# A triangular inverse packed to 64 columns a chunk, on quarters of the matrix engine

## What is computed

```
a_mat = jnp.where(strict, jnp.einsum("bnhid,bnhjd->bnhij", kb, kc) * gamma, 0.0)
lhs = a_mat + jnp.eye(c, dtype=a_mat.dtype)
rhs = jnp.concatenate([vc * bc[..., None], kb * jnp.exp(decay)[..., None]], axis=-1)
sol = lax.linalg.triangular_solve(lhs, rhs, left_side=True, lower=True, unit_diagonal=True)
```

## Time and profile before

| | us |
|---|---|
| median of 3 runs (1599.14 to 1600.18) | 1600.07 |
| the profiled execution | 1601.17 |
| its span on the core | 1599.4 |
| PE busy, share of the span | 1569.8 (98%) |
| DVE, ACT, POOL busy | 912.6, 687.6, 160.7 |
| granted clock, mean | 0.997 |
| the loop over units, first to last record on PE | 195.9 to 268.0 |

### The profile page before, as it was taken

How to read it: one execution, slowest core, us unless ns; L and a number is a source line. 1 busy time by engine, 2 the same in 40 slices (tenths; PEclk the granted TensorE clock), 3 DMA queues, 4 the chain that set the end, 5 groups by cost and what they waited for, 6 DMA issues and landing times.

```text
span 1599.4 us, 21522 instructions
## 1 busy us (share of the span) xinstructions
PE 1569.8 (98%) x7488; PEld 1303.5 (82%) x7488; DVE 912.6 (57%) x1318; ACT 687.6 (43%) x1001; POOL 160.7 (10%) x101
## 2 busy tenths in 40 slices
PE   6999999999999999999999999999999999999997
PEld 5888798888788888888788888888888888888886
DVE  5569887865754234443477666666456544444332
ACT  6735656554644223333255554444224434443221
POOL 3444585300000000000000000000000000000000
PEclk9999999999999999999999999999999999999998
DMA  7522100132132332322233333333232332232332
GB/s 271 187 80 67 54 1 28 40 106 79 45 114 92 105 99 85 103 98 88 82 96 95 96 97 98 99 99 106 93 104 79 106 103 93 92 105 78 101 97 79
DMA packets 45665, 149.50 MB, mean 93 GB/s; under 512 B 4784, under 2 KB 5936, under 8 KB 45616
## 3 DMA queue, kind: packets, MB, share of 16 engines
q1 hardware_dynamic: 42240, 139.90, 27.2%
q10 hardware_dynamic: 3376, 8.95, 1.6%
HBM read 146.47 MB, written 2.10 MB: 93 GB/s over the span
## 4 chain that ended last, share of the span: by engine, by line
PE 94%; DVE 3%; DMA 1%; ACT 1%; issue 0%; SPq 0%; DVEq 0%; ACTq 0%
PE acc L633 85%; DMA raw<-panels_a 1%; PE acc L878 1%; PE acc L918 1%; DVE c_acc L2127 1%; PE acc L890 1%; DVE w_lo L1995 1%; PE acc L1126 0%; PE acc L1147 0%; PE acc L807 0%; PE acc L949 0%; PE acc L708 0%; PE acc L974 0%; DVE x L2702 0%; DVE d_score_a L2219 0%
## 5 line engine op out<-in xcount | busy, mean ns | idle before, releaser
L633 PE MATMUL acc<-h_hi,w_hi 128*128 128x512 f32 x1248 | 491.3, 394 | 1.2 <-DVE w_lo L2003 0.7
L633 PE MATMUL acc<-h_hi,w_lo 128*128 128x512 f32 x1248 | 485.9, 389 | 0.0
L633 PE MATMUL acc<-h_lo,w_hi 128*128 128x512 f32 x1248 | 485.8, 389 | 0.0
L2003 DVE TENSOR_TENSOR w_lo<-raw,w_hi 128x1024 fp32r<-128x1024 f32 (+2 forms) x241 | 281.6, 1171 | 81.8 <-ACT w_hi L1397 57.7
L1397 ACT ACTIVATE w_hi<-raw 128x1024 fp32r<-128x1024 f32 (+2 forms) x241 | 242.0, 1008 | 177.2 <-PE acc L633 86.1
L633 PEld LDWEIGHTS acc<-h_hi,w_hi 128*128 128x128 f32 x1248 | 234.4, 188 | 51.6 <-issue 3.5
L633 PEld LDWEIGHTS acc<-h_hi,w_lo 128*128 128x128 f32 x1248 | 234.3, 188 | 49.1
L633 PEld LDWEIGHTS acc<-h_lo,w_hi 128*128 128x128 f32 x1248 | 234.5, 188 | 48.1 <-issue 1.0
L2405 DVE TENSOR_TENSOR x<-x,acc 128x512 f32 x32 | 22.0, 688 | 136.0 <-PE acc L633 135.5
L633 PE MATMUL acc<-u_hi,w_hi 128*128 128x512 f32 x256 | 99.6, 389 | 0.0
L633 PE MATMUL acc<-u_lo,w_hi 128*128 128x512 f32 x256 | 99.6, 389 | 0.0
(11 more groups left out here) (400 smaller groups left out, 2317.2 us busy)
## 6 DMA issues: line engine op xcount, KB each, us to landing
raw<-panels_a SPq DMA_DIRECT2D x112, 512.0 KB, 3.2
raw<-panels_b SPq DMA_DIRECT2D x68, 512.0 KB, 3.2
raw<-mix SPq DMA_DIRECT2D x48, 448.0 KB, 3.4
raw<-mix SPq DMA_DIRECT2D x16, 512.0 KB, 3.6
raw<-down SPq DMA_DIRECT2D x16, 384.0 KB, 3.1
raw<-down SPq DMA_DIRECT2D x16, 320.0 KB, 2.8
x<-xT ACTq DMA_DIRECT2D x4, 1024.0 KB, 9.5
x_rows<-xN ACTq DMA_DIRECT2D x2, 1024.0 KB, 9.3
```

The costliest lines, as they stand in the source:

```text
L633: mm = e.matmul(out, w[:, w_at:w_at + wn], a, start=first and n == 0, stop=last and n == 2)
L2003: TTn(lo, raw, k.w_hi[:, ahead.slot(w)].bitcast(F32), ALU.subtract).then_inc(k.s_split_done, 1)
```

## The change

The inverse is kept for its two diagonal blocks of 64 only, as long as the level is under 6: the block of rows 0 to 63 and the block of rows 64 to 127 lie in the same 64 columns, on their own partitions. So a head's X has 256 columns (g_xp), its transpose too (g_xtp), and so have A (g_ap) and the masked A (g_b).

- Products and updates for u < 20 are eight fp32 matmuls instead of four. Each has 64 rows and 64 weight columns and moves 32 columns; the two blocks of a chunk come one behind the other, on rows and output partitions 0 to 63 and then 64 to 127, into the same PSUM bank.
- The turn is eight ordinary fp32 matmuls with 64x64 of the identity instead of four transposes.
- The last level (u >= 20) takes A's corner block directly: its mask step on POOL goes away, its product is four 64x64 matmuls moving 64 columns, and so is its update.
- Elementwise work halves: the mask 128x256, the copy of P 128x128 (64x256 at the last level), the subtraction 128x128, the copy of the turned inverse 128x128 (128x256 at level 1, two of 64x256 at level 5).
- Added on ACT: eight 64x256 copies that pack A, ahead of L1586; the first X is taken out of PSUM in eight copies of 64x256 instead of four of 128x512.
- PE's order in iteration u becomes: `power_product(u+1)`, update(u), `turn_inverse(u-1)`, front(u), turned(u). ACT's order stays.

```diff
...
 
 REST, CKV, CQ, UG, Z = 0, 1, 2, 4, 8
 UNITS = (LEVELS - 1) * HEADS
+W64, LAST = TT * 64, (LEVELS - 2) * HEADS
 WT_BANKS, GO_BANKS = (6, 7, 1, 2), (2, 0, 2, 0)
 PAIRS, BEAT = TT * HEADS, 3
 
...
     "out_row ").split())}
 
 ACT_ONCE = {n: i + 1 for i, n in enumerate((
-    "xk_sq d_gates_tok beta_done sp_exp xk_std dec_exp k_root dk_raw d_std go_std aq_std ").split())}
+    "xk_sq d_gates_tok beta_done sp_exp xk_std dec_exp k_root at_packed dk_raw d_std go_std aq_std ").split())}
 
 DVE_ONCE = {n: i + 1 for i, n in enumerate((
     "sp_in xk_inv g_ready dec_copied br qe dv_done d_inv dk_done c_bias go_bias go_inv "
...
     k.w_hi, _ = sb("w_hi", SPLIT * PANEL, F32R)
     k.x, a = sb("x", KT * T)
     k.g_at, b = sb("g_at", HEADS * T, at=a - KT * T * 4)
-    k.g_b, _ = sb("g_b", 4 * T, at=b)
     k.g_o, _ = sb("g_o", HEADS * T, at=b)
+    k.g_b, _ = sb("g_b", 4 * W64, at=b)
     k.d_qi, b = sb("d_qi", 2 * T, at=b)
+    k.g_ap, b = sb("g_ap", HEADS * W64, at=b)
     k.const, _ = sb("const", NCONST)
     k.vec, _ = sb("vec", NVEC)
     k.eps, _ = sb("eps", 4)
...
     k.qkv, a = sb("qkv", 12 * T, at=r0)
     k.g_qk, a = sb("g_qk", HEADS * T, at=a)
     k.d_relu, _ = sb("d_relu", HEADS * T, at=a)
+    k.g_xp, b = sb("g_xp", HEADS * W64, at=a)
+    k.g_xtp, _ = sb("g_xtp", HEADS * W64, at=b)
     k.g_x, a = sb("g_x", HEADS * T, at=a)
     k.g_xt, a = sb("g_xt", HEADS * T, at=a)
     k.g_kdec, a = sb("g_kdec", HEADS * T, at=a)
...
     return ap.rearrange("p (b s) -> p b s", s=1 << lev)
 
 
+def rows64(b):
+
+    return slice(64 * b, 64 * b + 64)
+
+
+def diag(buf, h, b):
+
+    return til(buf, h)[rows64(b), :].rearrange("p (c t) -> p c t", c=TT)[:, :, rows64(b)]
+
+
 def til(buf, j, n=1, w=T):
 
     return buf[:, j * w:(j + n) * w]
...
     def masked(u):
 
         h, lev = u % HEADS, 1 + u // HEADS
-        mask = k.const[:, C_LEV + lev * P:C_LEV + (lev + 1) * P].unsqueeze(1).broadcast_to([P, TT, P])
+        mask = k.const[:, C_LEV + lev * P:C_LEV + lev * P + 64].unsqueeze(1).broadcast_to([P, TT, 64])
         if u >= 4:
             e.wait_ge(k.s_p_mm, u - 3)
         else:
-            e.wait_ge(k.s_at_done, h + 1)
+            e.wait_ge(k.s_act_once, ACT_ONCE["at_packed"])
             e.wait_ge(k.s_idx_mm, 3 * HEADS)
             e.wait_ge(k.s_ld_masks, 16)
-        TTn(til(k.g_b, u % 4).rearrange("p (c i) -> p c i", c=TT), til(k.g_at, h).rearrange("p (c i) -> p c i", c=TT),
-            mask, ALU.mult).then_inc(k.s_bt_done, 1)
+        TTn(til(k.g_b, u % 4, w=W64).rearrange("p (c i) -> p c i", c=TT),
+            til(k.g_ap, h, w=W64).rearrange("p (c i) -> p c i", c=TT), mask, ALU.mult).then_inc(k.s_bt_done, 1)
 
     def conv_add(n):
 
...
         if p >= first:
             conv_add(p - first)
     for u in range(UNITS):
-        masked(u)
+        if u < LAST:
+            masked(u)
         conv_add(early - first + u)
     for n in range(early - first + UNITS, CONV_PARTS):
         conv_add(n)
...
     e.wait_ge(k.s_dve_once, DVE_ONCE["dk_done"])
     def power_product(u):
 
-        h, b = u % HEADS, (u % 4) * T
-        e.wait_ge(k.s_bt_done, u + 1)
+        h, lev = u % HEADS, 1 + u // HEADS
+        if u < LAST:
+            e.wait_ge(k.s_bt_done, u + 1)
         if u < HEADS:
             e.wait_ge(k.s_x_first, u + 1)
         else:
             e.wait_ge(k.s_x_done, u - 3)
         if u >= 2:
             e.wait_ge(k.s_p_copied, u - 1)
-        lev = 1 + u // HEADS
         for c in range(TT):
-            at = c * P
-            mm = e.matmul(packed(k.ps[u % 2][:, c * 64:(c + 1) * 64], lev), k.g_b[:, b + at:b + at + P],
-                          halves(til(k.g_x, h)[:, at:at + P], lev)[:, 0], start=True, stop=True)
+            x = k.g_xp[:, h * W64 + c * 64:h * W64 + (c + 1) * 64]
+            if u >= LAST:
+                mm = e.matmul(k.ps[u % 2][rows64(1), c * 64:(c + 1) * 64],
+                              k.g_at[rows64(0), h * T + c * P + 64:h * T + (c + 1) * P], x[rows64(0), :], start=True, stop=True)
+                continue
+            for b in range(2):
+                mm = e.matmul(packed(k.ps[u % 2][rows64(b), c * 32:(c + 1) * 32], lev),
+                              k.g_b[rows64(b), (u % 4) * W64 + c * 64:(u % 4) * W64 + (c + 1) * 64],
+                              halves(x[rows64(b), :], lev)[:, 0], start=True, stop=True)
         mm.then_inc(k.s_p_mm, 1)
+
+    def update(u):
+
+        h, lev, at = u % HEADS, 1 + u // HEADS, (u % 2) * T
+        e.wait_ge(k.s_p_copied, u + 1)
+        if u >= 2:
+            e.wait_ge(k.s_x_done, u - 1)
+        if u >= HEADS:
+            e.wait_ge(k.s_xt_done, u - HEADS + 1)
+        if LAST <= u < UNITS - 2:
+            e.wait_ge(k.s_xt_done, u - 1)
+        for c in range(TT):
+            if u >= LAST:
+                mm = e.matmul(k.ps[4 + u % 2][rows64(0), c * 64:(c + 1) * 64], k.g_p[rows64(1), at + c * 64:at + (c + 1) * 64],
+                              k.g_xt[rows64(1), h * T + c * P + 64:h * T + (c + 1) * P], start=True, stop=True)
+                continue
+            for b in range(2):
+                if lev == 1:
+                    xt = k.g_xt[rows64(b), h * T + c * P + 64 * b:h * T + c * P + 64 * b + 64]
+                else:
+                    xt = k.g_xtp[rows64(b), h * W64 + c * 64:h * W64 + (c + 1) * 64]
+                mm = e.matmul(k.ps[2 + u % 2][rows64(b), c * 32:(c + 1) * 32], xt, k.g_p[rows64(b), at + c * 32:at + (c + 1) * 32],
+                              start=True, stop=True)
+        mm.then_inc(k.s_xp_mm, 1)
 
     def turn_inverse(u):
 
...
         if u >= 2:
             e.wait_ge(k.s_xt_done, u - 1)
         for c in range(TT):
-            at = c * P
-            mm = e.transpose(k.ps[4 + u % 2][:, at:at + P], til(k.g_x, h)[:, at:at + P], ident)
+            for b in range(2):
+                mm = e.matmul(k.ps[4 + u % 2][rows64(b), c * 64:(c + 1) * 64],
+                              k.g_xp[rows64(b), h * W64 + c * 64:h * W64 + (c + 1) * 64], ident[rows64(b), rows64(b)],
+                              start=True, stop=True)
         mm.then_inc(k.s_xt_mm, 1)
 
     power_product(0)
     for u in range(UNITS):
-        h, last, b = u % HEADS, u >= UNITS - HEADS, (u % 2) * T
         if u + 1 < UNITS:
             power_product(u + 1)
+        update(u)
+        if 1 <= u <= LAST:
+            turn_inverse(u - 1)
         front(*FILL[u])
         if u in TURNS:
             name, th, src = TURNS[u]
             turned(name, th, src, src + th + 1 if src == 8 else 1)
-        e.wait_ge(k.s_p_copied, u + 1)
-        if u >= 2:
-            e.wait_ge(k.s_x_done, u - 1)
-        if u >= HEADS:
-            e.wait_ge(k.s_xt_done, u - HEADS + 1)
-        if last:
-
-            if u < UNITS - 2:
-                e.wait_ge(k.s_xt_done, u - 1)
-            for c in range(TT):
-                at = c * P
-                mm = e.matmul(k.ps[4 + u % 2][0:64, c * 64:(c + 1) * 64], k.g_p[:, b + c * 64:b + (c + 1) * 64],
-                              til(k.g_xt, h)[:, at + 64:at + P], start=True, stop=True)
-        else:
-            for c in range(TT):
-                at = c * P
-                mm = e.matmul(k.ps[2 + u % 2][:, c * 64:(c + 1) * 64], til(k.g_xt, h)[:, at:at + P],
-                              k.g_p[:, b + c * 64:b + (c + 1) * 64], start=True, stop=True)
-        mm.then_inc(k.s_xp_mm, 1)
-        if 1 <= u <= UNITS - HEADS:
-            turn_inverse(u - 1)
     left("z3")
     left("kt3")
 
...
     leave("ckv", til(k.proj, CKV))
     round_lead()
     conv_part()
+    for h in range(HEADS):
+        e.wait_ge(k.s_at_done, h + 1)
+        for b in range(2):
+            ins = A(til(k.g_ap, h, w=W64)[rows64(b), :].rearrange("p (c t) -> p c t", c=TT), diag(k.g_at, h, b), ACT.Copy)
+    ins.then_inc(k.s_act_once, 1)
     e.wait_ge(k.s_pe_once, PE_ONCE["dk_mm"])
     A(k.d_rk[:], k.ps[4][:], ACT.Square).then_inc(k.s_d_sq, 1)
     A(k.d_k[0:64, :], k.ps[4][0:64, :], ACT.Copy)
...
     turned_value(0)
     for h in range(HEADS):
         e.wait_ge(k.s_x_turned, h + 1)
-        A(til(k.g_x, h), k.ps[h][:], ACT.Copy).then_inc(k.s_x_first, 1)
+        for b in range(2):
+            ins = A(til(k.g_xp, h, w=W64)[rows64(b), :].rearrange("p (c t) -> p c t", c=TT), diag(k.ps[h], 0, b), ACT.Copy)
+        ins.then_inc(k.s_x_first, 1)
     for u in range(UNITS):
 
         e.wait_ge(k.s_p_mm, u + 1)
         if u >= 2:
             e.wait_ge(k.s_xp_mm, u - 1)
-        A(k.g_p[:, (u % 2) * T:(u % 2) * T + T // 2], k.ps[u % 2][:, 0:T // 2], ACT.Copy).then_inc(k.s_p_copied, 1)
+        rows, n = (slice(0, P), P) if u < LAST else (rows64(1), W64)
+        A(k.g_p[rows, (u % 2) * T:(u % 2) * T + n], k.ps[u % 2][rows, 0:n], ACT.Copy).then_inc(k.s_p_copied, 1)
         if parts.at() < CONV_PARTS:
             conv_part()
         if FILL[u][2] == KT:
...
                 turned_value(h)
             else:
                 turned_key(h)
-        if 0 <= u - 2 < UNITS - HEADS:
-
```

(21 more changed lines are left out.)

## The result

| | before | changed |
|---|---|---|
| median of 6 runs | 1600.12 us | 1628.78 us |
| lowest to highest | 1599.14 to 1601.49 | 1609.49 to 1636.95 |
| ratio, 95% interval | | 1.0155 [1.0128, 1.0183] |
| the profiled execution | 1601.17 | 1631.03 |
| its span, granted clock | 1599.4, 0.997 | 1629.2, 0.978 |

The ratios and intervals, here and among the experiments, leave out runs over 1.5% above the fastest of the same kernel (here 1636.95); the medians keep them.

What follows compares the result with a forecast made beforehand. PE was taken to bound the kernel, carrying 94% of the chain. Start -0.5 and loop +5.0 made +4.5 on the profiled 1601.17, so 1605.7, or 1604.6 us for the median; range for 8 in 10: 1595.5 to 1616.

Steps and rivals of the forecast that it cites:

- What bounds the kernel, and the price of quarter work: Loop: PE carries 94% of the chain; product, update and turn 0.46 us each, plain unit 2.46 against 2.87.
- The switches: PE going from whole to part array and back in each unit: 0.30 us, bounds 0.1 and 0.5.
- the rivals in which the halves take turns: PE's quarter pairs: streams take turns, +7.4, 1612 us (15%); or no overlap at all, +22, 1627 us (8%).
- What the new order uncovers: Loop: PE waits behind ACT's bursts for P's copy; intervals 5.20 us at keys, 4.20 at values.
- the wait for z3's copy: Loop's end, after update(23) and front(23): PE waits for ACT's copy of z3, 0.16 + 0.69 us more.
- The sum at full clock: update(2) to L1044: 68.39 us against 63.39, 5.0 more.
- the wait for a turn copy in the last level: Placed at update(21), behind ACT's burst of u = 19, making u = 20 take 2.60 us.
- The start: Ahead of the loop: DVE saves 2.0 us, x(0) at 200.1, update(2) at 204.15, 0.5 earlier.
- What costs nothing: Eight packing copies on ACT, 2.4 to 3.4 us, hidden in its 7.47 us wait before L1586; shorter POOL and DVE work.
- the rival in which it falls: Loop: new waits drop PE to 1.2 GHz in the 11 plain units, +27, 1632 us; chance 3%.
- the prediction's own sign of being wrong: In the trace: the counted waits missing, a product's rows at 1.1 or more, or granted clock below 1.00 in the loop.
- Slower: Whole kernel: slower by over 3.2 us, 68%; within 21%, faster 11%.

Runs made afterwards that it cites:

- e4: Changed kernel plus useless whole-array fp32 matmuls on PE where it waits behind ACT's bursts of scaled copies; 1614.42 us, 1.0100 of before.
- e9: e8 plus e4's filler matmuls in PE's waits behind ACT's bursts; 1601.73 us, 1.0010 of before.
- e8: Changed kernel with front(0) ahead of the first product, front(1) ahead of update(0), last updates in banks 2 and 3; 1609.22 us, 1.0037 of before.
- e3: Changed kernel with ACT's scaled copies of a turned unit one iteration later, behind the copy of P; 1602.11 us, 1.0024 of before.
- e1: Changed kernel with PE's old order restored, packing and halved elementwise work kept; 1599.42 us, 0.9992 of before.
- e5: e1 with the last level's updates written to banks 2 and 3, not those of the turned inverse; 1591.14 us, 0.9939 of before.
- e6: e5 with front(0) ahead of the first product and front(1) ahead of update(0), where PE waited at the start; 1589.06 us, 0.9927 of before.
- e2: Kernel before with only the new PE order, matmuls still whole-array; 1621.73 us, 1.0132 of before.

## Why the prediction was wrong, point by point

- *What bounds the kernel, and the price of quarter work*: right. 0.46 to 0.48 for each product and update, 2.44 for a plain unit against 2.46. The switches cost less than taken: turn and front together took 1.49 where 1.54 was counted. The pairs overlapped although they write to one PSUM bank. That settles the rivals in which the halves take turns: with streams in turn a turn would have cost 0.39 on top of the 0.46 and its switch, and it took 0.59 with the switch. The rule of TensorEngine Tiling (Array Packing), section Gotcha 1: PSUM Pressure, of the Trainium skill, didn't bind for two row halves that write to different partitions of a bank.
- *What the new order uncovers*: right, with 2.01 us of wait at the key bursts of u = 10, 13 and 16 where 2.1 was counted, and 5.05 for 5.20; values 4.12 or 4.13 (e4, e9) for 4.20; the wait for z3's copy 0.69, as given.
- *The sum at full clock*: right, in part because misses cancel. e4 has the changed kernel's path with its clock at 1.00 from 205 on. In it update(2) begins at 206.51 and the old L1044 (its L1076) at 274.57: 68.06 us, where the sum has 68.39. One term was misplaced: the wait for a turn copy in the last level stands at update(20), not update(21). So u = 19 took 7.26 in e4 where 5.45 stood, and the other terms together 2.1 less than they were given. e8 and e9 at 0.997 or more took 1600.5 to 1604.6, where 1602 to 1604 was expected of e8.
- *The start*: DVE's six taps fell from 8.97 to 5.92, 3.05 saved where 2.0 was taken and 2.6 was the bound; the masks take 0.735 and not 0.64 (rows below). 0.81 of that went unused, because x(0) waited so long for update(0); it began at 199.86, where 200.1 was forecast. But update(2) began at 207.90 and not at 204.15, with the clock down from 198 on. What I left out is that product(0), product(1) and update(0) stand back to back in the new order, with ACT's copies between them, so PE waits twice there, 0.87 and 1.14 us.
- *What costs nothing*: right; the packing copies took 3.4 us at 147.0 to 150.4, in ACT's wait of the earlier trace rows.
- *The clock*: this is the step that failed. The sum put every piece and every wait at granted clock 1.00, and the rival in which it falls had 3%. I had no row of before with a wait over a microsecond in the loop, and read the missing evidence as if it spoke for a steady clock. What the runs showed in its place is granted clock 0.50 for 38, 10 and 16 us of the loop in the profiled execution; the prediction's own sign of being wrong, a clock below 1.00 in the loop, came. At full clock the change costs about 5 us, by two estimates: e4's profiled run had 1607.90 with some 7 us at half clock, worth 3, which leaves 1605; and the changed kernel's fastest run, 1609.49 at 0.994, comes to 1605.5 at 0.997 by the 21.5 us that went with 0.016 of clock. The changed kernel itself had no run at 0.997. The rest, some 24 us, is the clock.
- *The price of that rival*, "+27, 1632" against 1628.78, was near by luck: it let the clock fall in the 11 plain units alone and doubled their time. It fell in whole stretches instead, plain and turned units alike, and a plain unit took 1.78 times as long.
- *Slower*: right. The waits that the prediction counted make about 5 us of it, and they also let the clock fall, which the forecast didn't have.

Timeline and lines of the changed kernel for the start:

```profile
193.13 5.92 DVE L2169 SCALAR_TENSOR_TENSOR c_acc<-c_y,vec,c_acc 128x512 f32<-128x512 f32 x6
199.86 0.29 DVE L2294 TENSOR_TENSOR g_xp<-g_xp,acc 128x128 f32<-128x128 f32 x1 [0.81 <-PE acc L923]
```

```profile
L584 POOL TENSOR_TENSOR g_b<-g_ap,const x20: 722/735/1169, 190.3 to 264.5; 128x256 f32<-128x256 f32 x20
L1616 ACT ACTIVATE g_ap<-g_at x8: 400/414/418, 147.0 to 150.0; 64x256 f32<-64x256 f32 x8
```

What stays open is when the clock falls and how long it stays down beside quarter work. Alike waits did and didn't lower it: of the three of 2.01 us in the changed kernel's profile one did, one of 2.27 at e4's update(20) did not, and those of 2.37 and 2.53 at that place in e3 and e1 did. From the start of the new order it was low to about 204 in e4, to 207 in e3 and to 235 in the changed kernel; from the start of the old order, to 204 in e5 and to 214 in e1. With one profile of each this isn't told apart from chance.

## What to carry to other kernels

When an edit makes PE's work smaller, look at what its old work covered: where the clock fell behind a wait of 2 us beside quarter work, the 10 to 30 us at half clock behind it cost more than the wait itself. Price every new PE wait twice, at full clock and with the work behind it at half, and give the second a real chance unless the trace has waits of that length at full clock. If a wait can't be taken away, useful work moved into it (e6) is best, and even useless whole-array matmuls (e9) hold the clock and cost nothing.

## What the runs showed of the hardware

- Granted clock fell to 0.50 behind PE waits of 1.97 to 2.95 us in whole-array work (e2, all four), and came back within 3 to 7 us. Beside 64x64 work it fell behind waits of 0.87 and 1.14 at the start (changed), and in e5 behind one of 0.87 alone, and stayed low for up to 38 us; but it held through later waits of 0.81 to 1.08 (e8) and through two of 2.01 (changed).
- Two 64x64 fp32 matmuls on diagonal quarters ran side by side into one PSUM bank: 16 records in 0.47 us, 0.059 a pair, where 8 records on one quarter took about as long. At the last level a product on one off-diagonal quarter ran in between an update or a turn on others (L894 and L923 records alternate from 274.52 on).
- Whole time and mean granted clock of a run went together: 0.016 of clock (0.994 to 0.978) was 21.5 us of the changed kernel.
